# Gate-logit matmuls issued in slices between the steps of the mixers, with the logits kept in DRAM until the branch stage

## The chip, the cores and the metric

One core of a Trainium2 chip runs the whole program once. The metric is the device time of that core in microseconds (us). The engines are PE (TensorE, matrix multiplication), DVE (VectorE), ACT (ScalarE), POOL (GpSimd) and SP (SyncE, which only starts transfers here). Each has its own instruction stream and waits on semaphores that the others raise.

## What is computed

The reference is a decoder trunk of two equal layers, in float32, for 512 prompt positions and 8 sample positions that share the weights (520 columns in the kernel). Of one layer:

```
u = rms_norm(x, w_pre) @ w_in        # split in a_q ... d_dt, and gate (4 * 1024 columns)
o_a, o_b, o_c, o_d = four mixers of the projected columns   # each (tokens, 256)
g = sigmoid(gate)                    # (tokens, 4, 1024)
merged = g[0]*(o_a@w_br_a) + g[1]*(o_b@w_br_b) + g[2]*(o_c@w_br_c) + g[3]*(o_d@w_br_d)
x = x + rms_norm(merged @ w_out, w_post)
x = x + rms_norm(conv_ffn(rms_norm(x, w_pre2)), w_post2)
```

The mixers are A (sparse attention over the 128 best scored keys, 256 for the samples), B (stick-breaking attention), C (matrix memory with exponential gates) and D (state space scan). The gate logits depend on the normalised input alone and not on the mixers. They are used only when the branches are merged.

## The kernel before

All activations lie feature-major: 128 features on the partitions, 520 tokens along the row. A dense weight tile is 128 output features by 1024 inputs. To keep float32 accuracy, ACT copies the tile's leading part to WH (`split`, line 913), and another engine subtracts it to give the rest part WL: DVE (line 1219) for most tiles, POOL (line 1600) for the second part of the projection. The input has the same two parts, XH and XL. One tile is then 48 matmuls of 260 columns (`dense_split`, helper line 439): 8 chunks of the input, three products, two halves of the tokens. WH and WL hold two tiles, so the split of tile m waits until PE is done with tile m - 2.

The order of work is written out by hand in one function per engine, and semaphores tie the functions together. Per layer:

1. the norm; 29 projection tiles with the sample group's scores between them;
2. the mix: a stretch of short dependent steps. First the transposes to token-major (line 609), the causal convolution and the gates of C and D; then the eight recurrent updates of the sample states (lines 648 and 652); then a loop over v = 0..7 (the four heads of C, then the four of D; lines 664 to 717); then a loop over t = 0..3 which does, for each t, 128 queries of A and one head of B (lines 747 to 795). In the t loop PE also runs `cached_values`: matmuls of 2 and 4 columns (lines 501 and 506) on the cached value rows of the sample group, 8 stretches of 24 matmuls;
3. the gates and branches: 8 rounds, each of four gate tiles (32 in all) and the four branch products (line 823). ACT turns the logits straight out of PSUM into sigmoids (line 1123), and DVE multiplies and adds (line 1195);
4. the output projection (8 tiles), the norm, and the feed-forward part.

Weight tiles and cache records pass through a ring R of 4 slots in the order in which PE uses them. SP starts a load when the slot is free, that is when PE is done with the tile four places earlier. The buffers B1 to B3 of the mixers lie on the place of XL, so XL is computed once more at the end of the mix (POOL lines 1653 to 1655, DVE line 1525).

Of the kernel before, what the change touches and what calls it, by code (L numbers as in the profile page):

```python
# [10 lines left out]
L = 2  # L11
NPR = 512
NSM = 8
# [3 lines left out]
KD = DM // 128  # L17
# [16 lines left out]
AQ, AK, AV, IQ, SM, BQ, BK, BV, CQ, CK, CV, CO, DZ, XX, XB, XC = (  # L34
    0, 2, 3, 4, 6, 7, 9, 11, 13, 15, 17, 19, 21, 23, 25, 27)
NPROJ = 29
IKD = 29
NF = 31
MERGED = 23

# [32 lines left out]
HI_OF = [15, 16, 17, 18, 19, 20, 9, 10]  # L73
# [4 lines left out]
BY_POOL = NPROJ - CUT - 2  # L78
# [15 lines left out]
def trunk_kernel(nc, x_in, pages, consts, vecs, states, c_state, d_state, k_c, v_c,  # L94
# [9 lines left out]
    with ctx:  # L104
# [18 lines left out]
        with nc.sbuf_tensor("TM", [128, 11, NT, 128], f32) as TM:  # L123
            pass
        WH = sb("WH", [128, 2, SLOT], f32r)
        WL = sb("WL", [128, 2, SLOT], f32r)
        T = sb("T", [128, 11 * NT * 128 - 4 * SLOT])
        R = sb("R", [128, RING, SLOT])
        S = sb("S", [128, 5, TOK])
        with nc.sbuf_tensor("B1", [128, TRI_W], f32) as B1, nc.sbuf_tensor("B2", [128, TRI_W], f32) as B2, \  # L130
                nc.sbuf_tensor("B3", [128, TRI_W], f32) as B3:
            pass
# [5 lines left out]
        HS = sb("HS", [128, 2, NSM, 128])  # L138
        PT = sb("PT", [1, NSM * PAGES], mybir.dt.int32)
# [6 lines left out]
        MR = sb("MR", [4, 512])  # L146
# [14 lines left out]
        SS = sb("SS", [128, 24, 16])  # L161
# [12 lines left out]
        def bblock(i, first=0):  # L174
# [17 lines left out]
        xl_first = sig("first_chunks_rest_part_ready_again", 4)  # L192
        xl_again = sig("rest_part_ready_again", 4)
# [117 lines left out]

        g_sig = sig("gate_sigmoid", 32)
# [8 lines left out]
        stored = sig("outputs_stored", 0)  # L321
        act_own = sig("act_own", 0)
# [3 lines left out]
        FIRST = {"K": CUT, "V": NPROJ + NU, "gate": NPROJ + 2 * NU, "out": NPROJ + 2 * NU + 40,  # L326
                 "up": NPROJ + 2 * NU + 48, "down": NPROJ + 2 * NU + 92}

        full_at, at = [], [0] * RING
        for l in range(L):  # L330
            for n in range(tiles_per):
                cache = CUT <= n < CUT + NU or FIRST["V"] <= n < FIRST["gate"]
                at[(l * tiles_per + n) % RING] += 32 if cache else 16
                full_at.append(at[(l * tiles_per + n) % RING])
# [4 lines left out]
        def proj(c):  # L339

            return c if c < CUT else c + NU

        def tile_done(l, n):
# [4 lines left out]
        SPLIT = ([proj(c) for c in range(NPROJ)] + [FIRST["gate"] + 5 * (q // 4) + q % 4 for q in range(32)]  # L348
                 + [FIRST["out"] + d for d in range(KD)] + [FIRST["up"] + j for j in range(2 * JF)]
                 + [FIRST["down"] + t for t in range(JF)])  # L350
# [6 lines left out]
        def lo_ready(l, m):  # L357

            if CUT + 2 <= m < NPROJ:
# [1456 lines left out]
```

## Time and profile before

| | us |
|---|---|
| median of 3 runs | 2902.84 (2900.55 to 2903.84) |
| span of the profiled execution | 2897.5 |
| first layer: mix, from the first transpose to the end of the t loop | 302.1 to 705.0 |
| first layer: wait for XL | 705.0 to 711.0 |
| first layer: gates and branches | 711 to 955.8 |
| busy PE, DVE, ACT, POOL | 2551.8, 1373.6, 961.6, 230.7 |

The page gives no device time for the profiled execution beside its span. The median of the timed runs is 5.3 us above the span, and the times ahead are compared on that footing. The second layer repeats the first with the same steps: the same transposes begin there about 1433 us later. A busy PE is not PE at its full clock, so the granted clock has to be read beside each stretch.

### The profile page before, as it was taken

Reading aid. Unit: us, or ns where it says so; the run is one execution under the profiler, and the core shown is the slowest. Engines: PE = TensorE matmul, PEld = TensorE weight load, DVE = VectorE, ACT = ScalarE, POOL = GpSimd, SP = SyncE. Lnnn points to the kernel's source line nnn. Section 1 sums busy time; section 2 is a strip of 40 time slices with the busy share of each in tenths; the row PEclk is TensorE's granted clock in tenths of the full one; section 3 lists DMA queues with packets and bytes.
Section 4 is the critical chain, followed back from the end, with each engine's and each line's share of the span. In section 5 each row is a group of like instructions: output and inputs, shape, how many; then the busy total and the mean of one; then the engine's idle time right before and its main releaser. Section 6 shows DMA issues by size and latency. Waiting matters only on the chain. (4 is left out here: it accounts for less than half of the span.)

```text
span 2897.5 us, 41258 instructions
## 1 busy us (share of the span) xinstructions
PE 2551.8 (88%) x16456; PEld 2166.6 (75%) x16456; DVE 1373.6 (47%) x2125; ACT 961.6 (33%) x1396; POOL 230.7 (8%) x350
## 2 busy tenths in 40 slices
PE   6999487998999889999888995879989997999996
PEld 6658333766999879999885782346679997999895
DVE  3338454356333366663342475433563334666623
ACT  3122523332222345553230224332322223454521
POOL 0014132002000000000000132210020000000000
PEclk9999668667999999999999995776779999999998
DMA  3462100221222212222315420012212222222221
GB/s 148 121 192 77 37 1 25 66 66 59 88 88 88 80 52 95 89 95 81 108 59 159 147 73 26 1 42 70 63 62 88 88 80 66 74 95 88 89 88 59
DMA packets 84178, 229.90 MB, mean 79 GB/s; under 512 B 10386, under 2 KB 27794, under 8 KB 83090
## 3 DMA queue, kind: packets, MB, share of 16 engines
q1 hardware_dynamic: 71426, 204.16, 22.0%
q10 hardware_dynamic: 12560, 23.11, 2.5%
q8 instruction: 130, 2.13, 0.3%
q14 instruction: 62, 0.51, 0.1%
HBM read 216.68 MB, written 10.55 MB: 78 GB/s over the span
## 5 line engine op out<-in xcount | busy, mean ns | idle before, releaser
L439 PE MATMUL PS<-XH,WH 128*128 128x260 f32 x3616 | 749.5, 289 | 59.6 <-DVE XL L1195 34.9
L439 PE MATMUL PS<-XL,WH 128*128 128x260 f32 x3616 | 734.5, 285 | 4.1 <-issue 2.7
L439 PE MATMUL PS<-XH,WL 128*128 128x260 f32 x3616 | 733.9, 285 | 0.0
L1219 DVE TENSOR_TENSOR WL<-R,WH 128x1024 fp32r<-128x1024 f32 x240 | 294.3, 1226 | 852.2 <-ACT WH L913 851.8
L913 ACT ACTIVATE WH<-R 128x1024 fp32r<-128x1024 f32 x270 | 285.9, 1059 | 1017.0 <-PE PS L439 860.7
L439 PEld LDWEIGHTS PS<-XH,WH 128*128 128x128 f32 x3616 | 567.5, 191 | 69.7 <-issue 44.8
L439 PEld LDWEIGHTS PS<-XL,WH 128*128 128x128 f32 x3616 | 563.7, 190 | 4.5 <-issue 4.5
L439 PEld LDWEIGHTS PS<-XH,WL 128*128 128x128 f32 x3616 | 563.3, 191 | 0.0
L439 PE MATMUL PS<-FR,WH 128*128 128x260 f32 x1024 | 187.4, 285 | 0.0
L1198 DVE SCALAR_TENSOR_TENSOR S<-S,V 128x510 f32<-128x510 f32 (+1 forms) x176 | 132.1, 751 | 44.9 <-ACT S L1162 41.8
L439 PEld LDWEIGHTS PS<-FR,WH 128*128 128x128 f32 x1024 | 151.0, 190 | 0.1
L823 PE MATMUL PS<-F,R 128*128 128x260 f32 x512 | 117.4, 386 | 3.4 <-DVE F L1195 3.3
L506 PE MATMUL PS<-QB,R 128*128 128x2 f32 x512 | 110.5, 320 | 0.0
L823 PEld LDWEIGHTS PS<-F,R 128*128 128x128 f32 x512 | 93.7, 190 | 22.4 <-DVE F L1195 10.1
L506 PEld LDWEIGHTS PS<-QB,R 128*128 128x128 f32 x512 | 106.3, 288 | 0.0
L1600 POOL TENSOR_TENSOR WL<-R,WH 128x1024 fp32r<-128x1024 f32 x30 | 71.9, 2397 | 301.5 <-ACT WH L913 301.5
L870 PE MATMUL PS<-F,R 128*128 128x260 f32 x384 | 87.5, 383 | 0.8 <-PE PS L870 0.8
L1313 DVE MAX8 M<-T 8x8 f32<-8x1025 f32 x64 | 77.9, 1217 | 18.8 <-ACT T L956 16.6
L870 PEld LDWEIGHTS PS<-F,R 128*128 128x128 f32 x384 | 71.5, 190 | 11.7 <-issue 1.6
L1596 POOL TENSOR_SCALAR F<-F 128x1040 f32<-128x1040 f32 x2 | 6.5, 3231 | 910.7 <-ACT F L940 910.7
L474 PE MATMUL PS<-S,K 128*128 128x260 f32 x128 | 40.6, 468 | 42.5 <-ACT S L903 42.2
L1314 DVE MATCH_REPLACE8 T<-M,T 8x1025 f32<-8x1025 f32 x64 | 76.8, 1200 | 0.0
(302 smaller groups left out, 3029.8 us busy)
## 6 DMA issues: line engine op xcount, KB each, us to landing
R<-w_up SPq DMA_DIRECT2D x88, 512.0 KB, 3.3
R<-w_gate SPq DMA_DIRECT2D x64, 512.0 KB, 3.3
R<-w_proj SPq DMA_DIRECT2D x58, 512.0 KB, 3.4
R<-v_c SPq DMA_DIRECT2D x128, 192.0 KB, 2.4
R<-w_down SPq DMA_DIRECT2D x44, 512.0 KB, 3.3
R<-k_c SPq DMA_DIRECT2D x72, 256.0 KB, 3.2
R<-k_c ACTq DMA_DIRECT2D x56, 256.0 KB, 3.6
R<-w_br SPq DMA_DIRECT2D x16, 512.0 KB, 3.3
```

The lines of the kernel that those rows point to most:

```text
L439: i = mm(PS[:, bank + a, 0:HALF], p[:, w, k * 128:(k + 1) * 128], x[:, a * HALF:(a + 1) * HALF], start=first and p is WH and x is hi, stop ...
L474: i = mm(PS[:, 4 + a, 0:HALF], kc(C_ONE), S[:, k % 2, a * HALF:(a + 1) * HALF], start=k == 0, stop=k == KD - 1)
L506: ins = mm(PS[:, 3, o:o + 2], slot(l, n)[:, v0 + 128 + 128 * c:v0 + 256 + 128 * c], PA[:, 256 + 32 * j + 4 * b + 2 * c:256 + 32 * j + 4 * ...
L823: ins = mm(PS[:, 4 + 2 * (q % 2) + a, 0:HALF], slot(l, nb)[:, 256 * br + 128 * k:256 * br + 128 * k + 128], F[:, o + k, a * HALF:(a + 1) * ...
L870: ins = mm(PS[:, bank + a, 0:HALF], slot(l, n)[:, 128 * e:128 * e + 128], F[:, q, a * HALF:(a + 1) * HALF], start=k == 0, stop=k == JF - 1)
L913: do(A(WH[:, half(l, m), :], slot(l, SPLIT[m]), ACT.Copy), w_hi)
L1198: do(v_.scalar_tensor_tensor(out, a, sc, b, o0, o1), s)
L1219: v_.tensor_tensor(WL[:, half(l, m), :], slot(l, SPLIT[m]), WH[:, half(l, m), :].bitcast(f32), ALU.subtract).then_inc(w_lo.sem, 1)
L1313: do(v_.max(M8[0:8, :], T[0:8, 0:PAST + 1]))
L1314: do(v_.match_replace(T[0:8, 0:PAST + 1], M8[0:8, :], T[0:8, 0:PAST + 1], TAKEN))
L1596: do(g_.tensor_scalar(F[:, BQ:BQ + 2, :], F[:, BQ:BQ + 2, :], 0.125, None, ALU.mult), scaled)
L1600: g_.tensor_tensor(WL[:, half(l, m), :], slot(l, SPLIT[m]), WH[:, half(l, m), :].bitcast(f32), ALU.subtract).then_inc(w_lo_p.sem, 1)
```

## The change

The gate tiles leave stage 3. Each is cut into 16 steps (a half of the tokens by one input chunk, three matmuls), and a table says up to which step PE has run at each place of the mix (`fill`): 96 steps ahead of the v loop, 64 in it, 352 in the t loop. ACT copies each finished half out of PSUM into RB and splits further gate tiles (`drain`); POOL, and no longer DVE, makes the rest parts of all gate tiles (`follow`, `split_rest`); SP stores each half to a DRAM scratch GATES and, in the branch stage, reads the logits back into S, from which ACT takes the sigmoid. `cached_values` moves from the t loop to the v loop. The features of F are numbered anew so that B1 and B2 lie in F behind the value rows, B3 lies in the sample state HS, and XL keeps its contents, so the second computation of XL goes. Stores of the value rows and of HS get semaphores of their own, for which POOL and DVE wait before they write there. Several PSUM banks are reassigned, since banks 1 and 3 now belong to the gates. Two waits come with that: in the v loop the broadcast for v + 1 waits for C's result (`c_h`) at v = 2 and 4, and the sum for C's norm stands at the end of its step. The splits of the first two output tiles by DVE now stand behind the last branch sum.

```diff
+NG = 32
+BY_POOL = NPROJ + NG - CUT - 2
+
+STEPS = 16
+PRE = [0, 32, 48, 64, 72, 80, 96]
+LOOP = [96 + STEPS * (v // 2 + 1) for v in range(8)]
+SPENT = LOOP[-1]
+IN_T = [[24, 16, 28, 12], [24, 16, 32, 14], [24, 16, 38, 14], [24, 16, 42, 12]]
+TO_T = [[SPENT + sum(map(sum, IN_T[:t])) + sum(IN_T[t][:p + 1]) for p in range(4)] for t in range(NT)]
+assert TO_T[-1][-1] == STEPS * NG
+
+MIX = [("gate", q) for q in range(PRE[-1] // STEPS)]
+for v in range(8):
+    MIX += [("V", UPS * v + t) for t in range(UPS)]
+    MIX += [("gate", q) for q in range((LOOP[v - 1] if v else PRE[-1]) // STEPS, LOOP[v] // STEPS)]
+MIX += [("gate", q) for q in range(SPENT // STEPS, NG)]
+TILES = ([("proj", c) for c in range(CUT)] + [("K", u) for u in range(NU)]
...
+                def keep(n):
+
+                    if TILES[n][0] == "gate":
+                        q = TILES[n][1]
+                        for a in range(2):
+                            sp.wait_ge(*g_out.nth(l, 2 * q + a))
+                            sp.dma_start(GATES[l, q, :, HALF * a:HALF * (a + 1)],
+                                         RB[:, HALF * a:HALF * (a + 1)]).then_inc(g_stored[a].sem, 16)
+                for kind, i in MIX:
+                    n = AT[kind, i]
+                    if kind == "V":
+                        cached(sp, l, n, i, V_REC, v_c)
+                    else:
...
+                for a in range(2):
+                    sp.wait_ge(g_stored[a].sem, 16 * NG * (l + 1))
                 for d in range(KD):
-                    for br in range(4):
-                        tile(l, FIRST["gate"] + 5 * d + br, w_gate[l, 4 * d + br], 1024)
-                    tile(l, FIRST["gate"] + 5 * d + 4, w_br[l, d], 1024)
-                for d in range(KD):
-                    tile(l, FIRST["out"] + d, w_out[l, d], 1024)
+                    for q in range(4 * d, 4 * d + 4):
+                        if q >= 4:
+                            sp.wait_ge(*br_used.nth(l, q - 4))
+                        else:
+                            sp.wait_ge(*at_tr.nth(l, 12 + q))
...
+            def gates(l):
+
+                done = 0
+                for q in range(NG):
+                    m = NPROJ + q
+                    n = AT["gate", q]
+                    for a in range(2):
+                        for k in range(KD):
+                            if k == 0:
+                                if a == 0:
+                                    pe.wait_ge(*w_hi.nth(l, m))
+                                    pe.wait_ge(*lo_ready(l, m))
+                                if q:
+                                    pe.wait_ge(*g_out.nth(l, 2 * q - 2 + a))
+                            for p, x in ((WH, XH), (WH, XL), (WL, XH)):
+                                i = mm(PS[:, 1 + 2 * a, 0:HALF], p[:, half(l, m), k * 128:(k + 1) * 128],
+                                       x[:, k, a * HALF:(a + 1) * HALF], start=k == 0 and p is WH and x is XH,
+                                       stop=k == KD - 1 and p is WL)
+                            if k == KD - 1:
+                                i.then_inc((tile_used if a else gate_half).sem, 1)
+                            done += 1
+                            yield done
+
             for l in range(L):
...
+                def fill(upto):
+
+                    while gate_now[0] < upto:
+                        gate_now[0] = next(gate)
...
+                    if i == 7:
+                        fill(PRE[1])
+                    elif i == 9:
+                        fill(PRE[2])
...
-                    cached_values(l, 2 * t)
+                    fill(TO_T[t][0])
...
+            def evacuate(l):
+
+                for q in range(NG):
+                    for a in range(2):
+                        if a == 0:
+                            act.wait_ge(*gate_half.nth(l, q))
+                        else:
+                            act.wait_ge(*tile_done(l, AT["gate", q]))
+                        if l or q:
+                            act.wait_ge(g_stored[a].sem, 16 * (NG * l + q))
+                        do(A(RB[:, HALF * a:HALF * (a + 1)], PS[:, 1 + 2 * a, 0:HALF], ACT.Copy), g_out)
+                        if a:
+                            for nxt in SPLIT_NEXT[q]:
+                                split(l, NPROJ + nxt)
+                        yield 2 * q + a + 1
+
...
+                token_major(7)
+                drain(PRE[1])
+                for i in range(8, len(TO_TM)):
                     token_major(i)
+                drain(PRE[2])
...
-                    act.wait_ge(*tile_done(l, FIRST["gate"] + 5 * (q // 4) + q % 4))
-                    if q + 2 < 32:
-                        split(l, NPROJ + q + 2)
-                    if q >= 4:
-                        act.wait_ge(*br_used.nth(l, q - 4))
-                    do(A(halves(S[:, q % 4, :]), pair(2 * (q % 2)), ACT.Sigmoid), g_sig)
+                    act.wait_ge(g_back[q % 4].sem, 16 * (8 * l + q // 4 + 1))
+                    do(A(S[:, q % 4, :], S[:, q % 4, :], ACT.Sigmoid), g_sig)
...
+            def split_rest(l, m):
+
+                pool.wait_ge(*w_hi.nth(l, m))
+                g_.tensor_tensor(WL[:, half(l, m), :], slot(l, SPLIT[m]), WH[:, half(l, m), :].bitcast(f32),
+                                 ALU.subtract).then_inc(w_lo_p.sem, 1)
+                pool.wait_ge(*lo_ready(l, m))
...
-                for k in range(4):
-                    rest = T[:, 0:TOK]
-                    do(g_.tensor_scalar(rest, X[:, k, :], V[:, l, V_NPRE + k:V_NPRE + k + 1], None, ALU.mult))
-                    do(g_.tensor_tensor(rest, rest, RB[:, :], ALU.mult))
-                    do(g_.tensor_tensor(XL[:, k, :], rest, XH[:, k, :].bitcast(f32), ALU.subtract), xl_first)
-
-
-N_MID, N_END, N_ALL = 15, 17, 17
+                    follow(TO_T[t][3])
```

**ACT, from the transposed copies to the gate logs.** TM are the token-major copies, SMT the inputs of C's and D's gates, RB the copied gate logits, WH the leading part of a weight tile. Before:

```order
L982 ACTIVATE TM<-PS 128x512 [waits transposed,conv_activated]
L982 ACTIVATE TM<-PS 128x512 [waits transposed,token_major_ready] x5
L999 ACTIVATE SMT<-SMT 128x4x8 [waits gate_inputs_ready,token_major_ready]
L1000 ACT_TABLE_LOAD
L1000 ACTIVATE SMT<-SMT 128x4x8 [waits act_own]
```

Now, from the same place:

```order
L1097 ACTIVATE TM<-PS 128x512 [waits transposed,conv_activated]
L1097 ACTIVATE TM<-PS 128x512 [waits transposed,token_major_ready]
L1021 ACTIVATE RB<-PS 128x260 [waits gate_first_half_done,token_major_ready]
L1021 ACTIVATE RB<-PS 128x260 [waits tile_used,gate_logits_copied]
L1003 ACTIVATE WH<-R 128x1024 [waits tile_used,slot3_full,gate_logits_copied]
L1021 ACTIVATE RB<-PS 128x260 [waits gate_half0_stored,gate_first_half_done,weight_leading_part_ready]
L1021 ACTIVATE RB<-PS 128x260 [waits gate_half1_stored,tile_used,gate_logits_copied]
L1003 ACTIVATE WH<-R 128x1024 [waits tile_used,slot0_full,gate_logits_copied]
L1097 ACTIVATE TM<-PS 128x512 [waits transposed,weight_leading_part_ready]
L1097 ACTIVATE TM<-PS 128x512 [waits transposed,token_major_ready] x3
L1021 ACTIVATE RB<-PS 128x260 [waits gate_half0_stored,gate_first_half_done,token_major_ready]
L1021 ACTIVATE RB<-PS 128x260 [waits gate_half1_stored,tile_used,gate_logits_copied]
```

Three gate tiles' copies and splits, each of which waits for PE, now stand between the transposed copies and the gate logs.

**POOL, first round of the t loop.** The rows with HS or B of 128x128 mask a diagonal block. Before:

```order
L1641 AFFINE_SELECT B<-B 128x128 [waits index_scores_ready,state_weights_ready]
L1590 AFFINE_SELECT B<-B 128x128 [waits b_softplus_ready,index_scores_masked]
L1590 AFFINE_SELECT B<-B 128x128 [waits pool_own] x3
L1590 AFFINE_SELECT B<-B 128x128 [waits b_weights_exp,b_softplus_masked]
L1590 AFFINE_SELECT B<-B 128x128 [waits pool_own] x3
L1641 AFFINE_SELECT B<-B 128x128 [waits index_scores_ready,b_weights_masked]
```

Now:

```order
L1778 AFFINE_SELECT HS<-HS 128x128 [waits index_scores_ready,weight_rest_part_ready_by_pool]
L1708 AFFINE_SELECT F<-F 128x128 [waits b_softplus_ready,index_scores_masked]
L1708 AFFINE_SELECT F<-F 128x128 [waits pool_own] x3
L1714 TENSOR_TENSOR WL<-R,WH 128x1024 [waits weight_leading_part_ready,b_softplus_masked]
L1708 AFFINE_SELECT F<-F 128x128 [waits b_weights_exp,weight_rest_part_ready_by_pool]
L1708 AFFINE_SELECT F<-F 128x128 [waits pool_own] x3
L1714 TENSOR_TENSOR WL<-R,WH 128x1024 [waits weight_leading_part_ready,b_weights_masked]
L1714 TENSOR_TENSOR WL<-R,WH 128x1024 [waits weight_leading_part_ready,weight_rest_part_ready_by_pool] x3
L1778 AFFINE_SELECT HS<-HS 128x128 [waits index_scores_ready,weight_rest_part_ready_by_pool]
```

Five rest parts of gate tiles stand between the masks, each behind ACT's leading part.

**PE, first round of the branch stage.** `PS<-F,R` are branch products, `XH` and `XL` the gate tiles. Before:

```order
L823 MATMUL PS<-F,R 128x260 [waits slot1_full]
L823 MATMUL PS<-F,R 128x260 x7
L823 MATMUL PS<-F,R 128x260 [waits branch_merged]
L823 MATMUL PS<-F,R 128x260 x3
L823 MATMUL PS<-F,R 128x260 [waits branch_merged]
L823 MATMUL PS<-F,R 128x260 x3
L439 MATMUL PS<-XH,WH 128x260 [waits weight_rest_part_ready,weight_leading_part_ready,gate_sigmoid]
L439 MATMUL PS<-XH,WH 128x260
L439 MATMUL PS<-XL,WH 128x260 x2
```

Now, with the whole stage of this kind:

```order
L915 MATMUL PS<-F,R 128x260 [waits a_output_copied,b_output_copied,slot1_full,d_output_ready,c_output_ready]
L915 MATMUL PS<-F,R 128x260 x7
L915 MATMUL PS<-F,R 128x260 [waits branch_merged]
L915 MATMUL PS<-F,R 128x260 x3
L915 MATMUL PS<-F,R 128x260 [waits branch_merged]
L915 MATMUL PS<-F,R 128x260 x3
L915 MATMUL PS<-F,R 128x260 [waits branch_merged,slot2_full]
L915 MATMUL PS<-F,R 128x260 x3
```

The gate tiles between the rounds are gone, and the products wait only for DVE's sums. SP's stream at the same place, where S receives the stored logits:

```order
L447 DMA GATES<-RB 128x260 [waits gate_logits_copied] x6
L469 DMA S<-GATES 128x520 [waits a_probs_transposed,gate_half1_stored,gate_half0_stored]
L469 DMA S<-GATES 128x520 [waits a_probs_transposed] x3
L424 DMA R<-w_br 128x1024 [waits tile_used]
L469 DMA S<-GATES 128x520 [waits branch_merged] x4
L424 DMA R<-w_br 128x1024 [waits tile_used]
```

Each read behind the first four waits for the sum that frees its part of S.

## Rows read from the trace of the kernel before

**Rows 1.** The page: PE busy in the span, and its granted clock in 40 slices.
```profile
PE 2551.8 (88%) x16456; PEld 2166.6 (75%) x16456; DVE 1373.6 (47%) x2125; ACT 961.6 (33%) x1396; POOL 230.7 (8%) x350
...
PEclk9999668667999999999999995776779999999998
```

**Rows 2.** Windows of the first mix: stretch, length, busy PE, PEld, DVE, ACT, POOL, clock, DMA.
```profile
302.12:355.63 53.51, 18.31 (x85) 14.11 (x85) 27.68 (x75) 32.10 (x53) 2.10 (x2) 0.55 0.12 42
355.63:381.21 25.58, 22.45 (x32) 5.98 (x33) 21.12 (x19) 2.79 (x4) 14.14 (x10) 0.50 0.00 0
381.21:487.00 105.79, 89.00 (x284) 44.74 (x284) 39.30 (x58) 37.83 (x53) 29.57 (x96) 0.75 0.00 0
504.00:705.00 201.00, 185.21 (x740) 132.28 (x739) 102.55 (x260) 62.37 (x117) 25.90 (x47) 0.66 0.25 71
705.00:711.00 6.00, 0.07 (x1) 0.07 (x1) 4.05 (x12) 2.47 (x3) 1.48 (x2) 0.69 0.01 1
711.00:953.00 242.00, 240.35 (x1779) 230.85 (x1780) 85.41 (x98) 59.02 (x72) 0.00 (x0) 0.99 0.26 86
```

**Rows 3.** Windows of PE alone: length, busy (instructions), granted clock, DMA share, GB/s.
```profile
509.54:519.80 10.26, 10.26 (x50) 0.50 0.35 90
529.39:536.20 6.81, 6.81 (x49) 0.78 0.34 90
711.00:714.30 3.30, 3.30 (x16) 0.53 0.00 0
714.30:735.50 21.20, 21.20 (x178) 1.00 0.23 76
```

**Rows 4.** Waits of PE, 302 to 711 us: releaser, us in total, times, longest.
```profile
PE PS L609 <- ACT TM L982: 14.1, 6, 4.6
PE PS L648 <- POOL B L1615: 11.9, 4, 11.1
```

**Rows 5.** Timeline of PE: start, length, line, operands [idle before].
```profile
420.56 1.65 PE L678 MATMUL PS<-F 64*128 64x256 f32 x4 [2.98 <-DVE B L1195]
...
735.53 7.31 PE L823 MATMUL PS<-F,R 128*128 128x260 f32 x32
...
955.82 0.82 PE L439 MATMUL PS<-FR,WH 128*128 128x260 f32 x4
```

**Rows 6.** Groups by line, ACT and DVE, 711 to 953 us: count, busy, mean ns.
```profile
L913 ACT ACTIVATE WH<-R 128x1024 fp32r<-128x1024 f32 x32 | 33.9, 1058 | 173.9 <-PE PS L439 173.8
L1123 ACT ACTIVATE S<-PS 128x520 f32<-128x520 f32 x32 | 19.4, 606 | 9.5 <-PE PS L439 8.5
...
L1195 DVE TENSOR_TENSOR S<-S,PS 128x520 f32<-128x520 f32 x22 | 15.3, 696 | 8.4 <-PE PS L823 8.3
```

**Rows 7.** DMA issues: KB each, median us from issue to landing.
```profile
R<-w_gate SPq DMA_DIRECT2D x64, 512.0 KB, 3.3
R<-k_c SPq DMA_DIRECT2D x72, 256.0 KB, 3.2
```

**Rows 8.** Timeline of ACT ahead of the gate logs.
```profile
323.55 3.74 ACT L982 ACTIVATE TM<-PS 128x512 f32<-128x512 f32 x6
327.32 0.23 ACT L999 ACTIVATE SMT<-SMT 128x32 f32<-128x32 f32 x1
```

**Rows 9.** Groups by line, the splits by POOL: least, median, largest ns of one.
```profile
L1600 POOL TENSOR_TENSOR WL<-R,WH x30: 2341/2405/2411, 193.8 to 1713.2; 128x1024 fp32r<-128x1024 f32 x30
```

**Rows 10.** Timeline of ACT: one copy of 256 columns out of PSUM.
```profile
547.46 0.38 ACT L1108 ACTIVATE F<-PS 128x256 f32<-128x256 f32 x1 [0.84 <-PE PS L488]
```

**Rows 11.** Groups by form, 504 to 705 us: the last selection by DVE.
```profile
L1501 DVE MAX8 M<-B 128x8 f32<-128x512 f32 x16 | 11.1, 695 | 0.5
L1502 DVE MATCH_REPLACE8 B<-M,B 128x512 f32<-128x512 f32 x16 | 10.8, 675 | 0.0
```

**Rows 12.** DVE line 1313 over the span: the selection beside POOL splits.
```profile
L1313 DVE MAX8 M<-T x64: 1216/1217/1219, 195.7 to 1713.6; 8x8 f32<-8x1025 f32 x64
```

**Rows 13.** DVE line 1195, 362 to 370 us: sums beside POOL products.
```profile
L1195 DVE TENSOR_TENSOR CS<-CS,SS x2: 692/1282/1873, 362.9 to 367.8; 128x512 f32<-128x512 f32 x2
```

More of the change, by code:

```diff
@@ L77 @@
 CUT = 12
-BY_POOL = NPROJ - CUT - 2
+NG = 32
[13 more added lines that the diff above has]
+TILES = ([("proj", c) for c in range(CUT)] + [("K", u) for u in range(NU)]
+         + [("proj", c) for c in range(CUT, NPROJ)] + MIX + [("br", d) for d in range(KD)]
+         + [("out", d) for d in range(KD)] + [("up", j) for j in range(2 * JF)] + [("down", t) for t in range(JF)])
+AT = {tile: n for n, tile in enumerate(TILES)}
+SPLIT_NEXT = [[q + 2] if AT["gate", q + 2] == AT["gate", q] + 2 else [] for q in range(NG - 2)] + [[], []]
+IN_LOOP = [list(range((LOOP[v - 1] if v else PRE[-1]) // STEPS, LOOP[v] // STEPS)) for v in range(8)]
+IN_LOOP[7] += [LOOP[7] // STEPS, LOOP[7] // STEPS + 1]
+assert sorted([0, 1] + sum(SPLIT_NEXT, []) + sum(IN_LOOP, [])) == list(range(NG))
 class Signal:
@@ new lines, in _ @@
+                for kind, i in MIX:
[3 more added lines that the diff above has]
+                    else:
+                        tile(l, n, w_gate[l, i], 1024)
+                    keep(n - RING)
+                for d in range(2):
+                    tile(l, AT["br", d], w_br[l, d], 1024)
+                    keep(AT["br", d] - RING)
+                for n in range(AT["br", 2] - RING, AT["br", 0]):
+                    keep(n)
@@ L420, in _ @@
+                for d in range(2, KD):
+                    tile(l, AT["out", d], w_out[l, d], 1024)
                 for j in range(2 * JF):
-                    tile(l, FIRST["up"] + j, w_up[l, j], 1024)
+                    tile(l, AT["up", j], w_up[l, j], 1024)
                 for j in range(JF):
-                    tile(l, FIRST["down"] + j, w_down[l, j], SLOT)
+                    tile(l, AT["down", j], w_down[l, j], SLOT)
             sp.wait_ge(norm_out.sem, L * norm_out.per)
@@ L683, in _ @@
                         finish(ins, st_block)
[L684 to L689 removed]
+                    cached_values(l, v)
                     pe.wait_ge(*vu_ready.nth(l, v))
@@ L1050, in _ @@
                         decays(v + 1)
+                    for q in IN_LOOP[v]:
+                        split(l, NPROJ + q)
                     if v in (1, 3):
@@ L1224, in pre_norm @@
                 dve.wait_ge(*root_ready.nth(l, j))
+                if l or j:
+                    for a in range(2):
+                        dve.wait_ge(g_stored[a].sem, 16 * NG * (l + j // 2))
                 do(v_.reciprocal(RB[:, :], S[:, 3, :]))
@@ L1537, in _ @@
                 for d in range(KD):
-                    for m in range(4 * d + 2, 4 * d + 6):
-                        split(l, NPROJ + m)
-                        if m == 4 * d + 3 and d:
-                            merged_rest(d - 1)
+                    if d:
+                        merged_rest(d - 1)
                     for br in range(4):
```

278 lines of the change are left out of this document (154 added, 124 removed).

## The prediction

> **What bounds the kernel now.** I read the page first. PE is busy for 88% of the span, but its granted clock falls to 5 to 7 tenths in two stretches, which are the mixes of the two layers [rows 1]. So in the mixes PE is the busiest engine and yet slow. Then I read windows of the first mix [rows 2]. Up to 355.63 PE is busy for 18.31 of 53.51 us, at a clock of 0.55. In the updates of the sample states it is busy for 22.45 of 25.58 at 0.50, while DVE works for 21.12. In the v loop it is 89.00 of 105.79 at 0.75, in the t loop 185.21 of 201.00 at 0.66. Only the gates and branches run at 0.99, and there PE is busy for 240.35 of 242.00 us: that stage is bound by PE alone. The clock has two levels, 1.2 and 2.4 GHz. 0.50 is the lower one, and a mean between is a mixture.
>
> A stretch in which PE waits or runs small matmuls therefore costs twice, in idle time and in the clock. One stretch of `cached_values` shows it: 10.26 us at 0.50, 6.81 us at 0.78 [rows 3], so 5.1 to 5.3 us at the full clock. The waits of PE in the mix are mostly for the token-major copies of ACT (14.1 us in 6) and for POOL and DVE around the sample updates (11.9 in 4) [rows 4]; in the v loop they are pieces of 3 us behind DVE [rows 5].
>
> **Unit prices.** After its first 3.30 us at 0.53, PE ran 178 gate matmuls in 21.20 us at 1.00 [rows 3]: 0.119 us each, 0.36 for a step of three, 5.7 for a tile, 183 for 32 tiles. At the lower clock 3.30/16 gives 0.206 and 9.9 a tile. The work of the gates doesn't shrink. It moves from a stretch at full clock into stretches where it can cover idle time and where it may lift the clock. All that follows is for one layer. There are two.
>
> **Branch stage: -179.** It lasted from 710.9 (with its first tile at 711.00) to 955.8, where the first output matmul begins [rows 5]: 244.9. Of that, 8 rounds of products stay, each 7.31 [rows 5]: 58.5. What can pace them in PE's place? DVE does a product and a sum per branch, 8 operations of 0.70 a round [rows 6]: 5.6, below 7.31. The logits come back from DRAM: each of the 4 parts of S goes round in a read (3.2 to 3.3, the loads [rows 7]), a sigmoid (0.61 [rows 6]), two operations of 0.70 and some 0.6 of hand-overs, 5.8, or 1.45 per branch against PE's 1.83. So PE still paces it, with less cover. Should a read take twice as long, the cycle is 9.1, 2.3 a branch, +14. At the start some 2 us, since the last logits need a copy, a store and a read (about 7.5) while PE still has t = 3's products; at the end about 5: two operations of 0.70, the leading part 1.06, and the rest part of the first output tile by DVE, now behind the last sum. Together 66, against 244.9.
>
> **The second XL: -6.** Between 705 and 711 PE ran for 0.07 us [rows 2]. That wait goes, as XL stays. What is late next are the first read-backs, counted above.
>
> **Up to the sample updates: +24.** 96 steps (34.4 us) are put here, where PE idled for 35.2 of 53.5 us. But the idle time is not where the steps are. PE's idle time is spread behind each copy, 3.74 for six and then the gate logs at 327.3 [rows 8]. ACT's stream is in order, and the gate logs now stand behind the copies and splits of three gate tiles, so 48 steps of PE: 17 us, less nothing, since the transposes before them wait too. Sixteen more steps ahead of the row terms: 5 to 6. The start, with XH and WH to wait for: 2. If DVE's work is the longer chain here and hides half, +10; at the lower clock 96 steps cost 59 us and it is +35.
>
> **Sample updates: -2.** DVE bounds them (21.12 of 25.58). The steps ahead may leave the clock higher and save the small remainder of PE.
>
> **The v loop: +64.** Own work: 89.00 at 0.75 is 67 at the full clock. Added: 8 stretches of `cached_values`, 8 x 5.3 = 42, and four gate tiles, 23. That is 132 at full clock. I take a mean clock of 0.86, midway between 0.75 before and 1.00 of the gates, because the gate tiles stand in one piece while two thirds of `cached_values` keep their small matmuls: 154. Of 16.8 us idle before, steps and cached values fill most, but PE now waits for C's result twice and behind longer DVE and ACT queues: 16 stays. 170 against 106. Bounds: 0.95 and 12 idle give 151 (+45); the former 0.75 and 20 idle give 196 (+90).
>
> **The t loop: +23.** It loses the 8 stretches, of which each took 6.81 to 10.26 [rows 3], 72 in all. That leaves 113 at 0.66, or 75 at full clock. It gains 352 steps, 126: 201 at full clock. With so much dense work I take 0.93: 216, and 8 idle of 15.8 before, since the steps stand at the waits: 224 against 201. The 22 us of DVE's last selection (11.1 + 10.8 [rows 11]) have 58 to 66 steps, 21 to 24 us, beside them. The 17 us between 487 and 504 belong to DVE and are left as they are. Bounds: 0.98 and 6 idle give 211 (+10); 0.87 and 15 give 246 (+45).
>
> **ACT and POOL.** ACT gets 64 copies of 0.4 (0.38 for 256 columns [rows 10]) and keeps 32 splits of 1.06, 60 us in a mix where it was busy for 135 of 403. POOL gets 32 rest parts of 2.4 [rows 9], 77 us. A tile's chain, 0.4 + 1.06 + 2.4 and hand-overs, is 4.3, less than the tile's 5.7 on PE, so it holds while neither is late. DVE's sums with two inputs in SBUF took up to 1.87 instead of 0.69 beside POOL's products [rows 13]; its MAX8 of 1025 columns beside POOL's splits shows no such spread, 1216 to 1219 ns [rows 12]. If ten of DVE's operations a layer meet a split, that is up to 12 us. It is in the bounds and not in the sum.
>
> Sum: -179 - 6 + 24 - 2 + 64 + 23 = -76, two layers -152. The span of the profiled execution is 2897.5 and the median 5.3 above it; I take this difference as kept: **2750** beside 2902.84.
>
> **Two rules of the Trainium skill.** The skill's page "TensorE: Matmul & The Clock Gate", Part 1, says that a clock gate slows the array according to how busy PE has been. In [rows 3] PE is busy for all of 10.26 us, and its clock is 0.50 throughout, so here being busy wasn't enough; the measurement decides. By the rule alone the v loop, where PE would hardly idle, would run at the full clock: about 148 in place of 170, and the total 2706. The page "GPSIMD Engine Reference", section 1 (Specifications), says that POOL shares its SBUF interfaces with VectorE, with contention for DVE instructions that have two SBUF inputs. [Rows 13] agree by their 1873 against 692 ns. It speaks against this change, which puts POOL's splits beside the sums of the mixers; by it the sum would be some 12 us a layer less good, 2774.
>
> **Rivals.**
> A. The gates come too late at their places. ACT and POOL serve the mixers in order, so a half is copied or a rest part made only when they get to it. For it: four rest parts stand in one piece behind the last mask of a round, 4 x 2.4 = 9.6, and ACT was busy for 62 of the 201 us of the t loop. Against it: tiles ahead are split two early. At 16 places in the t loop, about 3 us each (a rest part and a hand-over), +46 a layer: **2842**.
> B. The clock stays near full and the steps sit where PE idled. For it: 1.00 within 3.3 us of the first gate tile [rows 3]. Against it: the cached values' 0.50. Each stretch at its lower end: +10 - 2 + 45 + 10 = 63 instead of 109, with the XL wait and the branches -122: two layers -244, and about 5 more where DVE and ACT start their next work sooner: **2655**. The skill's clock rule, named above, points this way.
> C. The clock falls, not rises. If the interleaved steps are too short a piece each to hold it, the gates' work is done at the mix's clock and not at 0.99. At full clock the mix after is 10 + 34 + 11 + 132 + 201 = 388 us of work, and the idle time in my sum is about 49 (with the 17). The mix may last 403 + 185 = 588 before the layer loses, so it decides at a mean clock of 388/539 = 0.72. The mix ran at 0.55 to 0.75 before [rows 2], which speaks for it; that 183 of the 388 are matmuls of the kind that ran at 1.00 speaks against it. At 0.55 the mix takes 705 + 49 = 754, +166 a layer: **3235**, slower.
> D. The read-backs bound the branch stage, at +14 a layer as worked out: **2778**. It lies within my own range.
> That the change does not do what it says I can't see: PE's stream has only products left between the sums of the branch stage.
>
> **Chances.** My forecast with D 0.61, A 0.15, B 0.18, C 0.06. The range takes in B's time and A's: 2650 to 2850. Outside it are C, some of B (lower still) and some of A. A measurement of this kernel tells 0.2%, about 6 us, from no change. Faster by more 0.92, within 0.02, slower 0.06.
>
> **What would show it.** The branch stage should last 62 to 80 us, with products of 7.31 in a row and waits for `branch_merged` of a few tenths. No 6 us gap should be there ahead of it. The mix should last about 512, at a granted clock of 0.8 to 0.9; the v loop 150 to 195 and the t loop 210 to 245. The gate logs of ACT should begin near 344 instead of 327. Waits of PE for ACT's copies or for POOL's rest parts of more than 20 us in a layer would be A; a clock below 0.72 in the mix C. The forecast is wrong if the mix grows by less than 80 or more than 140 us.

## Result and profile after

The changed kernel takes 2832.42 us (2818.8 to 2841.91, 4 runs) against 2903.34 us: ratio 0.975, 95% interval 0.9731 to 0.977. It is faster by 71 us, a little less than half of the 152 us that were forecast. The page of the changed kernel, with the lines of [rows 1]:

```profile
PE 2540.2 (89%) x16456; PEld 2175.6 (77%) x16456; DVE 1285.4 (45%) x2047; ACT 1013.4 (36%) x1526; POOL 348.1 (12%) x390
...
PEclk9999766769999899999999997676799998999998
```

The slices with a low clock are still there. Where they lie is seen in windows of PE alone (length, busy (instructions), granted clock, DMA share, GB/s). First the kernel before, in the bounds used from here on: mix up to the sample updates, the updates, the v loop with its last wait, the t loop up to the first branch product (with the gate tiles of round one).

```profile
302.10:355.60 53.50, 18.31 (x84) 0.55 0.12 42
355.60:381.20 25.60, 22.45 (x32) 0.50 0.00 0
381.20:492.70 111.50, 89.00 (x285) 0.76 0.00 0
499.00:735.50 236.50, 210.87 (x936) 0.69 0.25 71
```

The same stretches of the changed kernel, and the branch stage, which now begins where the t loop ends:

```profile
306.10:383.50 77.40, 54.52 (x372) 0.82 0.21 68
383.50:407.40 23.90, 19.25 (x33) 0.62 0.10 28
407.40:616.90 209.50, 191.44 (x861) 0.69 0.26 78
623.60:857.60 234.00, 222.29 (x1417) 0.94 0.28 83
857.60:923.00 65.40, 59.66 (x256) 0.99 0.63 194
```

| per layer | forecast | measured |
|---|---|---|
| branch stage | -179 | 65.4 for 244.9: -179.5 |
| up to the sample updates | +24 | +23.9 |
| sample updates | -2 | -1.7 |
| v loop | +64 | 209.5 for 111.5: +98.0 |
| t loop and the XL wait | +23 - 6 = +17 | 234.0 for 212.0 (499.0 to 711): +22 |
| sum | -76 | about -37 |

The gap is 39 a layer, and 34 of it are the v loop. Twice -37 is 16 more than the 57.7 by which the two profiled spans differ (2839.8 and 2897.5). Most of these 16 lie in stretches that the change doesn't address: the first mix begins 4.0 later, the way from the branch stage to the second mix takes 789 in place of 780. Part of that is scatter: the first mix began between 303.9 and 309.4 in the experiments, whatever was changed in them.

The branch stage is as forecast. Timeline of PE, changed kernel, answering to [rows 5]:

```profile
868.85 7.48 PE L915 MATMUL PS<-F,R 128*128 128x260 f32 x32 [0.24 <-DVE F L1315]
876.50 7.48 PE L915 MATMUL PS<-F,R 128*128 128x260 f32 x32 [0.17 <-DVE F L1315]
...
923.03 1.21 PE L497 MATMUL PS<-FR,WH 128*128 128x260 f32 x4 [4.46 <-issue]
```

The products follow each other with 0.2 us between rounds, and the cost at the end is 4.46. No wait for a read-back shows.

In the v loop PE waits little: 191.44 of 209.50 us are busy. But busy at which clock? 191.44 x 0.69 is 132 us of work at full clock, which is the forecast's 132. So its size was right and the clock was not: 0.69 against the 0.86 that I took. Single stretches of the changed kernel show it, first and second `cached_values` (the first and third row) with the gate tile between them:

```profile
421.44:431.77 10.33, 10.33 (x49) 0.50 0.34 107
439.70:445.52 5.82, 5.82 (x48) 1.00 0.00 0
449.12:457.90 8.78, 8.78 (x48) 0.58 0.44 128
```

(The trace has two records for each fp32 matmul, so that the 24 matmuls of a stretch show as 48.) The gate tile runs at the upper level (2.4 GHz), and the cached values behind it are soon back at the lower one. The gate tile did not carry them.

### The profile page after: what moved, and what is told of

The parts are those of the page before. It is cut to its first block and busy times, and to the rows that moved or that the text cites. A ratio compares the mean times of both kernels' runs of the same rounds, so it can differ in the third digit from the quotient of the medians.

```text
span 2839.8 us, 41630 instructions
## 1 busy us (share of the span) xinstructions
PE 2540.2 (89%) x16456; PEld 2175.6 (77%) x16456; DVE 1285.4 (45%) x2047; ACT 1013.4 (36%) x1526; POOL 348.1 (12%) x390
## 5 line engine op out<-in xcount | busy, mean ns | idle before, releaser
L497 PE MATMUL PS<-XH,WH 128*128 128x260 f32 x2592 | 540.2, 290 | 47.9 <-DVE XL L1315 36.3
L497 PE MATMUL PS<-XL,WH 128*128 128x260 f32 x2592 | 529.2, 286 | 4.3 <-issue 2.8
L497 PE MATMUL PS<-XH,WL 128*128 128x260 f32 x2592 | 528.1, 285 | 0.0
L1339 DVE TENSOR_TENSOR WL<-R,WH 128x1024 fp32r<-128x1024 f32 x176 | 215.7, 1226 | 555.9 <-ACT WH L1003 555.6
L497 PEld LDWEIGHTS PS<-XL,WH 128*128 128x128 f32 x2592 | 406.3, 192 | 4.7 <-issue 4.7
L497 PEld LDWEIGHTS PS<-XH,WL 128*128 128x128 f32 x2592 | 405.7, 192 | 0.0
L582 PE MATMUL PS<-XH,WH 128*128 128x260 f32 x1024 | 304.8, 298 | 16.5 <-ACT RB L1021 16.3
L1714 POOL TENSOR_TENSOR WL<-R,WH 128x1024 fp32r<-128x1024 f32 x94 | 223.3, 2376 | 730.8 <-ACT WH L1003 729.9
L582 PE MATMUL PS<-XL,WH 128*128 128x260 f32 x1024 | 298.3, 291 | 0.0
L582 PE MATMUL PS<-XH,WL 128*128 128x260 f32 x1024 | 297.0, 290 | 0.0
L582 PEld LDWEIGHTS PS<-XH,WL 128*128 128x128 f32 x1024 | 202.1, 197 | 0.0
L582 PEld LDWEIGHTS PS<-XL,WH 128*128 128x128 f32 x1024 | 202.0, 197 | 0.0
L1021 ACT ACTIVATE RB<-PS 128x260 f32<-128x260 f32 x128 | 49.6, 387 | 246.8 <-PE PS L582 144.7
L915 PE MATMUL PS<-F,R 128*128 128x260 f32 x512 | 119.4, 388 | 4.5 <-DVE F L1315 3.1
L915 PEld LDWEIGHTS PS<-F,R 128*128 128x128 f32 x512 | 94.4, 190 | 29.1 <-DVE F L1315 9.8
```

The lines of the kernel that those rows point to most:

```text
L497: i = mm(PS[:, bank + a, 0:HALF], p[:, w, k * 128:(k + 1) * 128], x[:, a * HALF:(a + 1) * HALF], start=first and p is WH and x is hi, stop ...
L582: i = mm(PS[:, 1 + 2 * a, 0:HALF], p[:, half(l, m), k * 128:(k + 1) * 128], x[:, k, a * HALF:(a + 1) * HALF], start=k == 0 and p is WH and ...
L915: ins = mm(PS[:, 4 + 2 * (q % 2) + a, 0:HALF], slot(l, nb)[:, 256 * br + 128 * k:256 * br + 128 * k + 128], F[:, o + k, a * HALF:(a + 1) * ...
L1021: do(A(RB[:, HALF * a:HALF * (a + 1)], PS[:, 1 + 2 * a, 0:HALF], ACT.Copy), g_out)
L1339: v_.tensor_tensor(WL[:, half(l, m), :], slot(l, SPLIT[m]), WH[:, half(l, m), :].bitcast(f32), ALU.subtract).then_inc(w_lo.sem, 1)
L1714: g_.tensor_tensor(WL[:, half(l, m), :], slot(l, SPLIT[m]), WH[:, half(l, m), :].bitcast(f32), ALU.subtract).then_inc(w_lo_p.sem, 1)
```

## Experiments

Two theories at the start. S: the matmuls of 4 and 2 columns hold the clock down wherever they stand. W: the v loop's clock is low by its own waits and short steps. The times are medians; ratios are to the kernel before, with their 95% intervals. In the cuts of code `page` stands for the part of the ring slot that is read, and `...` for arguments left out.

**e1, other columns.** Instructions, weights and places stay; only the columns differ.

```diff
-mm(PS[:, 7, 448 + 4 * b:...], page[128], PA[:, 4 columns])    # and two of 2 columns
+for c in range(3):
+    mm(PS[:, 7, 408:512], page[128 * c:...], PA[:, 32 * j:32 * j + 104])
```

> The changed kernel, but each of the 24 matmuls of a cached_values stretch moves 104 columns (of PA) where it moved 4 or 2; the cached output is therefore another. The instructions, their weights and their places are the same, only the columns differ. Theory S (the small matmuls hold the clock down, and it stays down for some us behind them): the stretches run near the full clock, 4 to 5.5 us each in place of 7 to 10.3; the granted clock of the v loop rises from 0.68 to 0.85 or more; the v loop takes about 165 us in place of 209, and the total is near 2750. Rival W (the v loop's clock is low by its own waits and its state blocks, whatever the cached values move): the clock stays within 0.03 of 0.68, the v loop takes 200 us or more, the total is above 2815.

2755.64 us, ratio 0.9505 (0.9481 to 0.9529). The v loop, and from the timeline its first and its last stretch of cached values:

```profile
411.30:580.40 169.10, 149.52 (x861) 0.87 0.32 97
```
```profile
425.33 8.82 PE L558 MATMUL PS<-QB,R 128*128 128x104 f32 x48
...
564.39 5.50 PE L558 MATMUL PS<-QB,R 128*128 128x104 f32 x48
```

Its first two stretches as windows, and the last stretch of the changed kernel, with 4 and 2 columns:

```profile
425.33:434.08 8.75, 8.75 (x49) 0.61 0.29 91
449.04:456.20 7.16, 7.16 (x50) 0.76 0.40 123
```
```profile
599.21:605.00 5.79, 5.79 (x51) 0.92 0.81 246
```

The loop took 169.10 us at 0.87, 40 us less. S is borne out and W's numbers fall. But the columns aren't all of it: the first stretches ran at 0.61 and 0.76 with 104 columns too, the last of the changed kernel at 0.92 with 4 and 2. The early ones stand behind C's state blocks, whose matmuls use 64 and 4 of the 128 partitions, and behind its waits; the late ones behind D's, with 128. Which of these holds the clock down there was not tried. 26 to 52 times as many columns cost almost nothing: 5.50 us for a stretch at full clock, where 4 and 2 columns would take 5.1 to 5.3. The two v loops give 81 us; the whole difference to the changed kernel is 77.

**e2, pieces between the state blocks.**

```diff
                         finish(ins, st_block)
-                    cached_values(l, v)
+                        cached_values(l, v, [i])
```

> The changed kernel, but the four units of cached_values (6 matmuls each) of a step v stand one behind each of the four state blocks, and no longer in one stretch behind them. Theory S: pieces of 1.3 us between matmuls of up to 512 columns pull the clock down less, 0.68 goes to 0.75 or more, and the units cover the 3.5 us waits behind DVE; the v loop falls from 209 to about 185, the total to about 2785. Rival W: the clock stays at 0.68, only some of the 12 us of idle time goes, the v loop takes 198 to 205 and the total is 2810 to 2825. A third outcome: DVE gets its state blocks later and the idle time grows, the v loop takes over 209.

2812.12 us, ratio 0.9685 (0.9669 to 0.9701).

```profile
409.50:605.90 196.40, 189.72 (x860) 0.70 0.28 84
```

The idle time falls from 18.1 to 6.7 us, the clock stays at 0.70. Here W's total came true (its loop of 198 to 205 nearly), for another reason: cutting the stretch up doesn't change what PE does on the whole.

**e3, the kernel before with this part alone.**

```diff
-                    cached_values(l, 2 * t)        # and 2 * t + 1, in the t loop
+                    cached_values(l, v)            # behind the state blocks of the v loop
```

> The kernel before with one part of the change alone: cached_values stands in the v loop (bank 7) and no longer in the t loop, and its result is read ahead of the t loop; no gate step is moved. Theory S: the v loop's clock falls from 0.75 to 0.60 or less, it takes about 111 + 75 = 186 us; the t loop loses 72 us and its clock rises from 0.66 to 0.75 or more, so it takes about 120; the total is within 2880 to 2905. Rival W: the v loop's clock stays at 0.75 and it grows by 8 stretches of 7 us less what covers idle time, to about 160; the t loop keeps 0.66 and takes 130; the total is about 2850.

3029.66 us, ratio 1.0438 (1.0419 to 1.0458): slower by 127, outside both ranges. v loop and t loop:

```profile
383.50:569.90 186.40, 167.65 (x669) 0.66 0.24 71
576.20:800.90 224.70, 143.32 (x552) 0.70 0.05 16
```

The v loop took just S's 186, at 0.66 and not below 0.60. The t loop was wrong in both theories: 67.6 us less work of PE made it 11.8 shorter. Its waits (releaser, us in total, times, longest):

```profile
PE PS L770 <- POOL B L1592: 36.0, 4, 10.1
PE PS L782 <- POOL B L1592: 19.4, 4, 5.1
```

Without the cached values PE stands idle for POOL's masks, so in the kernel before they had been a cover and nearly free. Moved alone they cost 75 in one loop and give back 12 in the other. It takes the gate steps to use the room they leave.

**e4, eight gate tiles in the v loop.** 64 steps fewer in the t loop.

```diff
-LOOP = [96 + STEPS * (v // 2 + 1) for v in range(8)]
+LOOP = [96 + STEPS * (v + 1) for v in range(8)]
```

> The changed kernel with eight gate tiles in the v loop, one behind every step v, and 64 steps less in the t loop (places 20-12-22-10, 20-12-26-12, 20-14-30-12, 20-14-34-10). Theory S: a tile behind every stretch of small matmuls lifts the clock for what follows; the v loop's clock rises from 0.68 to 0.75 or more, so that four more tiles (23 us at full clock) add only about 15 us, the t loop loses 24, the total is about 2815. Rival W: the v loop's clock rises only by the tiles' own share, the v loop takes 209 + 24 to 34, the t loop loses 24, the total is 2832 to 2850.

2810.5 us, ratio 0.9682 (0.9653 to 0.9711), near S's total. Its v loop, then its t loop:

```profile
408.00:624.30 216.30, 207.98 (x1053) 0.74 0.29 89
630.20:844.60 214.40, 199.21 (x1224) 0.94 0.25 76
```

Four more tiles, 23 us of work, made the loop 6.8 longer, and the t loop 19.6 shorter. S's reason holds in part only. Of the 16 us that the loop saves, 9.7 are idle time (18.1 before, 8.3 now), which the tiles cover; the other 6.5 are the clock's.

**e5, steps alternate with small matmuls.** The same work as e4, and an edit of a few more lines so that a slot of the ring is given back at the first matmul of a gate tile.

```diff
                         j, v0 = 2 * t + jj, V_REC * jj
+                        fill(LOOP[b] - STEPS + 2 * j + 2)    # two steps, then three small matmuls
```

> The changed kernel with eight gate tiles in the v loop (as e4_eight_tiles), and their steps no longer behind a stretch of cached_values but inside it: two gate steps (6 matmuls of 260 columns, 0.72 us at full clock) ahead of every three small matmuls (0.64 us). For this a gate tile's slot is given back at its first matmul, and its end has a signal of its own. All the work of e4 is there. Theory S, in the form that what counts is how long PE runs small matmuls without dense ones: the stretches run at 0.9 or more, the v loop's clock rises from 0.74 (e4) to 0.88 or more, the v loop takes about 185 in place of 216, the total is about 2750. Rival P (the clock falls with the share of small matmuls, however they are arranged): the v loop keeps 0.74 to 0.78 and takes 205 or more, the total is 2790 to 2812.

2915.34 us, ratio 1.0026 (1.0013 to 1.004): the whole gain is gone, and both theories missed. The v loop, then a piece of its second stretch:

```profile
413.10:677.80 264.70, 236.46 (x1052) 0.65 0.24 74
461.46:474.90 13.44, 13.44 (x63) 0.50 0.25 78
```

236.46 x 0.65 is 154, and e4's 207.98 x 0.74 is 154: the same work. The loop is 48.4 us longer than e4's. Of these, 28.5 are busy time at a lower clock; 19.9 are idle time (28.2 against 8.3, in waits for DVE and ACT), which the clock doesn't explain: the edit also moves ACT's copies, POOL's splits and the order of SP's loads and stores. In the piece the clock is 0.50 throughout, in the gate steps too. The timeline there, the last matmul of two steps (each takes 0.21 from start to start there, as at the lower level in [rows 3]) and the small ones behind it:

```profile
462.69 0.42 PE L591 MATMUL PS<-XH,WL 128*128 128x260 f32 x1
462.91 0.42 PE L566 MATMUL PS<-QB,R 128*128 128x4 f32 x2
463.19 0.99 PE L571 MATMUL PS<-QB,R 128*128 128x2 f32 x4
```

The dense steps don't lift the small matmuls; the small ones drag the dense steps down. What first brings the clock down in this stretch isn't shown: it falls at 459.96, in the first gate steps and ahead of the first small matmul, behind 3.59 us of C's state blocks (64 and 4 partitions) at 1.00. What e5 shows is that the mixture doesn't bring it up again. S holds in another form than I had given it. Small matmuls are to stand apart, so that only they are slow.

**e6, the same between the state blocks.** e5 with e2's edit.

> As e5_alternate, and the four units of a step v (each with its four gate steps) stand one behind each state block, so that they also cover the waits behind DVE. Theory S: the idle time of the v loop falls below 8 us, the v loop takes about 178, the total is about 2740. Rival P: the clock is that of e4 (0.74 to 0.78), only the idle time goes, the total is 2780 to 2805. If the state blocks come so late that DVE's sums bound the loop, idle time behind DVE is above 15 us.

2854.93 us, ratio 0.9868 (0.9802 to 0.9935), above both ranges; v loop 230.1 us, 12.8 of them idle, clock 0.72. The state blocks' matmuls of up to 512 columns are part of the mixture now, which may be why the clock is higher than in e5. It is better than e5 and still worse than tiles in a piece.

**e7, two tiles ahead of the v loop in place of six.**

```diff
-PRE = [0, 32, 48, 64, 72, 80, 96]
+PRE = [0, 32, 32, 32, 32, 32, 32]
```

> The changed kernel with only two gate tiles ahead of the v loop in place of six; the other 64 steps go to the t loop (places 32-20-32-16, 28-20-36-18, 28-20-42-18, 26-20-46-14). By the prediction's term for that stretch (steps there delay ACT's gate logs, so they cost nearly their whole time: 17 to 23 us for these 64) the stretch falls from 77 to about 57 and the t loop grows by 64 x 0.36 / 0.94 = 24.5, so the total is 2832 to 2845. Rival: the steps ahead of the v loop cost more than they save elsewhere, for ACT's copies and splits stand in its chain too, and the stretch falls by 28 or more: the total is 2815 to 2828.

2851.44 us, ratio 0.9821 (0.9804 to 0.9837). The stretch ahead of the updates and the t loop:

```profile
304.90:365.40 60.50, 31.97 (x181) 0.65 0.17 55
602.50:859.90 257.40, 241.47 (x1609) 0.97 0.30 88
```

-16.9 ahead and +23.4 in the t loop, against 17 to 23 and 24.5: the prediction's term for that stretch has the right size, and the total is 6 above the range given. Steps ahead are worth having, if barely. These two stretches make 13 us of the 19 between the medians. The v loop, in which nothing was changed, was 4.4 us a layer shorter in this profile; it is of e7's fastest execution, and that of the changed kernel is of its slowest.

**e8, e2 and e4 together.**

> e2_between and e4_eight_tiles together: units of cached_values one behind each state block, one gate tile in a piece at the end of every v, 64 steps less in the t loop. Theory S: both gains add up, since one breaks up the small matmuls and covers waits (20 us in all) and the other puts dense work behind them (22 us): about 2790. Rival P: they overlap and the total stays at 2800 to 2812.

2808.91 us, ratio 0.9674 (0.9658 to 0.9691): P. They overlap. The v loop is busy for 212.26 of 215.20 us at 0.74, so little is left to gain by covering waits.

**e9, 104 columns with the reference's result.**

```diff
+                        o = 260 + 4 * (7 - b)
+                        mm(PS[:, 1, o:o + W], page, PA[:, 32 * j + 4 * b:32 * j + 4 * b + W], ...)
+                            o = 380 + 118 * c + 2 * b      # wanted columns last, b from 7 to 0
+                            ins = mm(PS[:, 3, o - W:o], page, PA[:, x - W:x], ...)
```

> A version of e1_wide that computes the reference: the changed kernel, with each matmul of cached_values moving 104 columns of PA, of which 4 or 2 are the wanted ones and the others fall on columns of banks 1 and 3 that are not read (or are written anew later); the samples are taken from the last to the first for this, PE waits for the last gate copy ahead of a stretch, and the result is read from banks 1 and 3. Theory S (the columns that PE moves over some time set its clock): as e1, v loop near 169 us at a clock of 0.87, stretches of 7.2 us, total 2750 to 2765. If the waits for the gate copies cost more than 2 us each, the total is above 2780.

2758.51 us, ratio 0.949 (0.9475 to 0.9506), v loop 169.10 us at 0.87, as in e1. The order of the samples, two banks and a wait per stretch differ from the changed kernel here, beside the columns.

**e10 and e11, with e2's edit, at 104 and 64 columns.**

```diff
-                W = 104
+                W = 64        # e11
```

> As e9, with the units of cached_values one behind each state block as in e2. Theory S: with no loss of clock the 18 us that PE still waits in the v loop fall to about 6, v loop about 158, total about 2735. Rival: the waits in e1 were what let DVE keep up, and the total stays at 2750 to 2765.

> As e10 with 64 columns in place of 104. If 64 columns still hold the clock, a stretch takes about 5.7 us in place of 7.2, v loop near 147, total near 2712. If they don't, the v loop's clock falls below 0.78 and the total is 2770 or more.

2750.29 us, ratio 0.9465 (0.9449 to 0.9481), and 2774.35 us, ratio 0.9547 (0.9531 to 0.9562). The v loops, e10 and then e11:

```profile
410.90:577.90 167.00, 157.16 (x861) 0.87 0.34 98
```
```profile
406.60:583.80 177.20, 167.46 (x860) 0.81 0.31 93
```

e10's total is at the edge of its rival's range and not at S's 2735: the wait time fell by 10, but PE was busy for 8 us more, and the loop is 2 us shorter. That more is not accounted for. With 64 columns the clock is 0.81, between the two cases of e11, and the total is the worse case's (2770 or more): fewer columns save nothing, they cost 10 us a layer. v loop by columns, with e2's order: 0.70 at 4 and 2, 0.81 at 64, 0.87 at 104.

**e12, the kernel before with 104 columns.** Its cached values stay in the t loop.

```diff
-mm(PS[:, 3, 4 * b:...], page[128], PA[:, 4 columns])    # and two of 2 columns
+for c in range(3):
+    mm(PS[:, 3, 0:104], page[128 * c:...], PA[:, 32 * j:32 * j + 104])
```

> The kernel before, where each matmul of cached_values (in the t loop there) moves 104 columns of PA; its cached output is another. Theory S: the t loop's clock rises from 0.69 to 0.82 or more, its 201 us fall to about 175, total about 2850. Rival: in the t loop the chain of POOL, ACT and DVE, for whose waits the cached values are only a cover (e3: 55 us of waits for POOL without them), bounds; the clock rises but the total stays above 2885.

2870.94 us, ratio 0.9877 (0.9861 to 0.9894), between the two.

```profile
503.80:723.30 219.50, 180.86 (x937) 0.81 0.26 76
```

The clock rises from 0.69 to 0.81, the stretch falls by 17.0 a layer and no more, since 38.6 us of it are idle now, and 25.6 were before. With wide matmuls on both sides the change is worth 2870.9 - 2758.5 = 112 us, with small ones 71.

**e13, e10 with eight tiles.**

> e10_columns_104_between with eight gate tiles in the v loop, one behind every v, and 64 steps less in the t loop, as in e4 and e8. With small matmuls the four more tiles paid 22 us, since they lifted the clock of the v loop from 0.69 to 0.74 and that loop grew by 7 us only. If that lift was made good on the small matmuls alone, it is gone here: the v loop (clock 0.87) grows by 4 x 5.7 = 23 to 25 us, the t loop falls by 20 to 24, and the total stays at 2744 to 2758. If dense tiles lift the clock of the rest of the loop as well (0.87 to 0.92 or more), the loop grows by 12 us or less and the total is 2725 to 2738.

2739.57 us, ratio 0.9434 (0.9415 to 0.9453).

```profile
407.10:589.90 182.80, 175.88 (x1053) 0.92 0.34 106
594.70:809.40 214.70, 200.03 (x1224) 0.94 0.25 76
```

Between the two cases: the v loop grows by 15.8, the t loop falls by 18.8. The mean clock rises from 0.87 to 0.92, where four more tiles at 1.00 and nothing else would give 0.88 to 0.89. So more dense tiles also lift what the loop does besides, and they cover 2.9 us of idle time (9.8 to 6.9); together this is less than with small matmuls. This is the fastest version, 93 us below the changed kernel.

## Why the prediction was half right

- The direction, the branch stage (-179), the updates and the stretch ahead of them came as worked out, and e7 confirms the price of steps there. ACT's gate logs began at 345.7, where 344 was forecast (327.3 before; this mix begins 4.0 later). The mix as a whole passed the prediction's own sign of being wrong: it grew by 148.6 us (551.5 below for 402.9), and more than 140 was named.

```profile
306.10:857.60 551.50, 491.36 (x2689) 0.81 0.25 76
```

- **The step that failed is the clock of the v loop.** The prediction put: "I take a mean clock of 0.86, midway between 0.75 before and 1.00 of the gates". That was no reading of a row. [Rows 3] had the cached values at 0.50 and at 0.78, and 42 of the 132 us were to be such matmuls, with the gate steps only 23. A price from the rows would have been 8 stretches of 6.81 to 10.26, 54 to 82, beside the loop's own 89 at its former clock, 23 for the gate tiles and 22.5 of idle time (111.5 less 89.0): 189 to 217. The measured value is 209.5. The upper bound of this term (196, +90) was too low for the same reason: it kept 0.75 for a loop into which the slowest matmuls of the mix were moved. This makes 68 of the 81 us that are missing. e1, where only the columns differ, gives 77 back, and e9 74.
- The Trainium skill's page "TensorE: Matmul & The Clock Gate", Part 1, ties the clock to how busy PE is. The v loop of the changed kernel is busy for 191.44 of 209.50 us (91%) at 0.69, that of e1 for 149.52 of 169.10 (88%) at 0.87. So this case's traces don't agree with being busy as the measure: it doesn't tell these two apart, their columns do.
- The t loop was 5 us a layer worse than forecast. The clock (0.94) and the idle time were as said; its full-clock work is 222.29 x 0.94, about 209, and not 201. Some 5 of these 8 are an error in the sum: it took 72 us of busy time off and then the mean clock (113 x 0.66 = 75), but the cached values ran below that mean. All work less theirs is 185.21 x 0.66 - 42 = 80. The other 3 stay open. My reading that it had 72 us of cached values "to lose" was wrong by itself, as e3 shows: they covered waits. The gate steps took over that cover, so that the term came out near, by luck and not by its reason.
- Rival A did not come: PE waits 7.9 us for gate copies in the mix and never for a rest part. Rival C did not come either: the gate tiles of the v loop ran at 1.00 (5.82 us above) and not at the mix's clock, and the mix's mean, 0.81, is above its 0.72. What was slow in the v loop (0.69) were the cached values and the steps around them.
- POOL's splits did cost DVE something, about 4 us in the first layer, where up to 12 were set aside. In the v loop no DVE instruction ran beside one of the six splits there, so this has no part in its 98. But two that read SBUF alone took longer elsewhere: the scan for the gates, beside a split that began at 363.22, and a multiplication by a scalar of 256 columns in the t loop, shown with the split beside it. Changed kernel:

```profile
363.80 2.86 DVE L1491 TENSOR_TENSOR_SCAN SROW<-SROW 4x512 f32<-4x512 f32 x1 [9.46 <-ACT SROW L1123]
712.32 2.48 DVE L1321 TENSOR_SCALAR HS<-HS 128x256 f32<-128x256 f32 x1
712.29 2.36 POOL L1714 TENSOR_TENSOR WL<-R,WH 128x1024 fp32r<-128x1024 f32 x1 [0.15 <-ACT WH L1003]
```

The same two in the kernel before:

```profile
337.67 1.21 DVE L1368 TENSOR_TENSOR_SCAN SROW<-SROW 4x512 f32<-4x512 f32 x1 [1.73 <-ACT SROW L1004]
L1201 DVE TENSOR_SCALAR B<-B x4: 228/326/428, 518.2 to 687.3; 128x128 f32<-128x128 f32 x1, 128x256 f32<-128x256 f32 x1, 128x384 f32<-128x384 f32 x1, 128x512 f32<-128x512 f32 x1
```

The scan's delay reaches PE: PE's wait for DVE's gate inputs behind it grew from 7.0 to 8.7 us. In e7, where no split stands there, the scan took 1.21 and the wait 7.1. DVE's MAX8 of 512 columns beside splits in the t loop kept its 0.70, and so did the sums that read PSUM.

## What to carry to other kernels

Multiply a stretch's busy time by its granted clock before moving work into it, and give a moved instruction the clock of the rows in which it ran, not a mean of its new neighbours. Matmuls of a few columns cost their own time and the clock: give them more columns when these are free in time (here 104 took 5.50 us for 5.1 to 5.3), or keep them in a piece; strewn among dense matmuls they slow these too. Before an instruction is moved away, ask what it covered where it stood.

## Hardware behaviour that was not expected

- Six gate matmuls in a row (1.45 us), alternating with three small ones (1.13 us), run at 0.50 for 13.44 us without a break, though PE never idles (e5).
- The changed kernel's runs scatter by 0.8% (2818.8 to 2841.91), those of e13 by 0.13% and those of before, beside it in the first comparison, by 0.2%. Their mean clocks are 0.895 to 0.902 in the first. What sets this from run to run was not tried.
